# Another layout of the expert lists over the partitions, and another order of POOL's three indirect DMAs

## What is computed

```python
def expert_step(acc, xs):
    wg, wu, wd, g = xs
    h = jax.nn.silu(t @ wg) * (t @ wu)
    return acc + (h @ wd) * g[:, None].astype(t.dtype), None
```

## Time and profile before

| | |
|---|---|
| median of 3 runs | 1410.04 us (1409.48 to 1410.26) |
| the profiled execution | 1410.28 us, its span 1408.4 us |
| PE busy | 1203.7 us, 85% of the span |
| DVE, ACT, POOL busy | 749.5, 529.0, 541.7 us |
| moved by DMA | 329.66 MB, mean 234 GB/s |
| the expert loop (PE's L1870) | about 617 to 1343 us |

### The profile page before, as it was taken

How to read it: one execution, slowest core, us unless ns; L and a number is a source line. 1 busy time by engine, 2 the same in 40 slices (tenths; PEclk the granted TensorE clock), 3 DMA queues, 4 the chain that set the end, 5 groups by cost and what they waited for, 6 DMA issues and landing times. The chain is left out here.

```text
span 1408.4 us, 16199 instructions
## 1 busy us (share of the span) xinstructions
PE 1203.7 (85%) x6611; PEld 950.5 (67%) x6611; DVE 749.5 (53%) x925; ACT 529.0 (38%) x707; POOL 541.7 (38%) x352
## 2 busy tenths in 40 slices
PE   7999788899999999659888988899898888988930
PEld 6999567899998984247666666666666666666620
DVE  3125793532125436337666666666666666666637
ACT  3223672522223120035444444444444444444411
POOL 2001441210010203825555555555555555555413
PEclk9999896899999979979999999999999999999975
DMA  9930601023224075338999999999999998999751
GB/s 276 225 99 29 218 2 68 31 76 104 62 90 178 1 282 208 104 140 329 349 354 347 355 352 348 335 354 356 358 360 359 354 346 344 343 344 350 292 173 69
DMA packets 106017, 329.66 MB, mean 234 GB/s; under 512 B 26866, under 2 KB 59812, under 8 KB 80708
## 3 DMA queue, kind: packets, MB, share of 16 engines
q1 hardware_dynamic: 74848, 265.28, 51.0%
q0 software_dynamic: 30384, 63.02, 13.8%
q10 hardware_dynamic: 708, 0.28, 0.1%
HBM read 324.71 MB, written 49.74 MB: 266 GB/s over the span
## 5 line engine op out<-in xcount | busy, mean ns | idle before, releaser
L838 POOL DMA_INDIRECT yg<-y_rows,idx_all x64 | 258.1, 4033 | 166.4 <-DMA y_rows<-yg,idx_all 160.5
L1510 DVE TENSOR_TENSOR wgu_lo<-wgu,wgu_hi 128x4096 fp32r<-128x4096 f32 x64 | 282.8, 4418 | 0.0
L1125 ACT ACTIVATE wgu_hi<-wgu 128x4096 fp32r<-128x4096 f32 x63 | 227.9, 3617 | 95.4 <-DMA wgu<-in_w_up_e_dram 95.3
L1889 PE MATMUL bank<-wd,hT 128*128 128x512 f32 x512 | 230.1, 592 | 1.3 <-DVE yg L1522 1.3
L1870 PE MATMUL bank<-wgu_hi,xgT 128*128 128x512 f32 x512 | 206.8, 404 | 0.0
L1870 PE MATMUL bank<-wgu_lo,xgT 128*128 128x512 f32 x512 | 201.1, 393 | 0.0
L1870 PE MATMUL bank<-wgu_hi,xgT_lo 128*128 128x512 f32 x512 | 200.3, 391 | 0.0
L1889 PEld LDWEIGHTS bank<-wd,hT 128*128 128x128 f32 x512 | 96.7, 189 | 98.4 <-issue 92.0
L1522 DVE TENSOR_TENSOR yg<-yg,bank 128x512 f32<-128x512 f32 x128 | 82.3, 684 | 149.4 <-PE bank L1889 149.4
L1858 PE MATMUL bank<-ident,xg 128*128 128x128 f32 x512 | 75.1, 291 | 100.0 <-DMA xg<-x_rows,idx_all 97.9
L1502 DVE TENSOR_TENSOR xgT_lo<-bank,xgT 128x512 fp32r<-128x512 f32 x128 | 82.5, 686 | 144.7 <-ACT xgT L1119 144.7
(11 more groups left out here) (274 smaller groups left out, 2263.4 us busy)
## 6 DMA issues: line engine op xcount, KB each, us to landing
wgu<-in_w_gate_e_dram SPq DMA_DIRECT2D x64, 1024.0 KB, 10.2
wgu<-in_w_up_e_dram SPq DMA_DIRECT2D x64, 1024.0 KB, 21.0
wd<-in_w_down_e_dram SPq DMA_DIRECT2D x64, 1024.0 KB, 14.3
raw<-in_w_in_dram SPq DMA_DIRECT2D x16, 1024.0 KB, 5.7
y_rows<-sgln POOLq DMA_DIRECT2D x8, 512.0 KB, 7.1
raw<-in_w_proj_a_dram SPq DMA_DIRECT2D x4, 1024.0 KB, 5.0
raw<-in_w_out_dram SPq DMA_DIRECT2D x4, 1024.0 KB, 4.9
x_lo_kept<-xT_lo SPq DMA_DIRECT2D x1, 2304.0 KB, 10.0
```

Of the source, the lines that this page charges most:

```text
L838: pool.indirect_dma_start(out=yg[i][:], out_offset=None, in_=y_rows[i], in_offset=bass.IndirectOffsetOnAxis(idx, 0), bounds_check=bound, o ...
L1125: act.activation(wgu_hi[u % 2][:], wgu[u % WSLOTS][:], ACT.Copy).then_inc(hi_by_act, 1)
L1510: v.tensor_tensor(wgu_lo[u % WSLOTS][:], w_[:], wgu_hi[u % 2][:].bitcast(F32), ALU.subtract).then_inc(lo_by_dve, 1)
L1889: last = mm(bank[3 + h][:, :], hT[:, u % 2, j, :], wd[slot][:, j, h * 512:(h + 1) * 512], start=j == 0, stop=j == FE // P - 1)
```

## The change

The view `spread` is rearranged: place `s * 64 + q * 16 + c * 2 + h` of a list now goes to partition `h * 64 + s * 32 + c * 4 + q` (`s` and `h` 0 or 1, `q` 0 to 3, `c` 0 to 7). So `idx_all` is loaded in four DMAs of 32 partitions, one for each `h` and `s`, where it was one DMA on POOL (and 16 on SP in the second path). The semaphores' counts follow. On POOL the step's order becomes: gather x of expert `e + 3`, gather y of expert `e`, scatter y of expert `e - 1`, each with the wait that it had.

```diff
-SPREAD = 16
...
-    spread = owner.rearrange("(t b a e) x -> t a b (e x)", t=NT, a=SPREAD, e=E)
+    spread = owner.rearrange("(t s q c h e) x -> t h s c q (e x)", t=NT, s=2, q=4, c=8, h=2)
+    QUARTERS = [(h, s, h * 64 + s * 32) for h in range(2) for s in range(2)]
...
-                    for a in range(SPREAD):
-                        sp.dma_start(idx_all[a * P // SPREAD:(a + 1) * P // SPREAD, :], spread[tile][a]).then_inc(idx_again, 16)
+                    for h, s, p0 in QUARTERS:
+                        sp.dma_start(idx_all[p0:p0 + 32, :], spread[tile][h][s]).then_inc(idx_again, 16)
...
-            pool.dma_start(idx_all[:, :], spread[0]).then_inc(idx_landed, 16)
+            for h, s, p0 in QUARTERS:
+                pool.dma_start(idx_all[p0:p0 + 32, :], spread[0][h][s]).then_inc(idx_landed, 16)
...
-            pool.wait_ge(idx_landed, 16)
+            pool.wait_ge(idx_landed, 64)
...
             for e in range(E):
-                if e >= NACC:
-                    pool.wait_ge(y_put[acc[e]], 16 * (turn[e] - 1))
-                gather_y(acc[e], idx_all[:, e:e + 1])
                 n = e + XGSLOTS - 1
                 if n < E:
                     if e >= 1:
                         pool.wait_ge(h_by_dve, e)
                         pool.wait_ge(ex_xt, e)
                     gather_x(n % XGSLOTS, xg_in[n % XGSLOTS], idx_all[:, n:n + 1])
+                if e >= NACC:
+                    pool.wait_ge(y_put[acc[e]], 16 * (turn[e] - 1))
+                gather_y(acc[e], idx_all[:, e:e + 1])
                 if e >= 1:
                     pool.wait_ge(y_by_dve, 2 * e)
                     scatter_y(acc[e - 1], idx_all[:, e - 1:e])
...
-                    v.wait_ge(idx_again, 16 * SPREAD * tile)
+                    v.wait_ge(idx_again, 64 * tile)
```

## The result

The changed kernel takes 1318.35 us (median of 4 runs, 1317.11 to 1319.55) against 1410.15 us for the kernel before in the same comparison: a ratio of 0.9343, 95% interval 0.9321 to 0.9365. The forecast was 1335 with a range from 1318 to 1372, so the time lies at the very edge of the range (0.9343 of the 1410.28 us from which the forecast starts is 1317.6, just outside it), and the gain of 91.8 us is 16.5 more than the 75.3 forecast. The profiled execution took 1319.55 us, 90.7 less than the one before.

A forecast was written before the change was run, and what follows sets the result against it. The prediction took eight of sixteen DMA engines, each carrying eight rows of each kind, as the bound. From 1410.28 us it took 77.3 for the loop, added 2.0 for the start and 0 for POOL's order: 1335 us, range 1318 to 1372.

The forecast's parts named there:

- the flat rate: Expert loop, from slice 19 on: 329 to 360 GB/s almost without change, read as DMA possibly setting the pace.
- the half-rate stretches: Inside a loop step, 414 GB/s alternates with 221 and 229, read as about half the engines having run dry.
- the sum of 297 KB: Load per step of an engine with eight rows: 196.6 KB weights plus 100.4 KB rows, 11.34 us at 26.2 GB/s.
- the 10.25 us a step: Expert loop with the new layout: 10.1 for DMA plus 0.15 for delays, bounds 10.01 and 10.9; gain 77.3 us.
- The start: Loading the lists ahead of the loop in four issues instead of one: +2.0 us, bounds 0 and +4.
- The POOL order: Gather of x issued 6.7 us sooner in each loop step: cost 0, bounds 0 and 17 us, adding cover.
- The branch that the prediction priced at 17 us: DVE's L1510 stretches x's issue to 4.4 us, so y lands 0.3 us late, 17 us over the loop.
- The landings: Gathers in the loop expected to land 4.6 to 8.4 us after issue with lists spread evenly; then nothing waits.
- Weights late: Rival: gathers take turns with weights on every engine, the loop's step settles at 10.8 us, 1366 us; chance 0.15.
- A rate limit of the memory: Rival: the core is limited to about 360 GB/s, so a loop step takes 11.25 us, 1392 us; chance 0.07.
- The other way round: Rival: an engine owns eight neighbouring partitions, so the new layout is the uneven one, slower at 1526 us; chance 0.04.
- no effect of the layout: Rival: engines not assigned by partition; earlier x gather alone brings 11.34 us a step at best, 1397 us; chance 0.04.

The follow-up runs named there:

- e3: Changed kernel with two of the list's four quarters exchanged, so places 0 to 63 lie on partitions 0 to 63: 1402.02 us, ratio 0.9951 to the kernel before.
- e4: Changed kernel with lists of partitions 4-7 and 32-35 exchanged, meant to give one engine eight of the first 64 places, another none: 1422.12 us.
- e7: Changed kernel with two four-partition groups' lists exchanged, meant to load the neighbour of the otherwise tested engine with eight places: 1424.58 us.
- e6: Kernel before with PE's third gate and up pass (8 of 24 matmuls) left out, all transfers kept: 1391.64 us, ratio 0.988.
- e2: Kernel before with POOL's new order per step (x gather, y gather, scatter), old layout kept: 1400.69 us, ratio 0.9937.
- e5: Changed kernel with PE's third gate and up pass (8 of 24 matmuls) left out, all transfers kept: 1297.42 us, ratio 0.9186 to the kernel before.

## Why the prediction was right and wrong

**What bounds the kernel before: right.** The prediction read eight loaded engines out of the flat rate, the half-rate stretches and the sum of 297 KB. The runs show it: the step follows the busiest engine's rows (e3, e4, e7), not PE's work (e6) and not the order (e2). One slip in it changes no term: the new layout does not put place k on engine k modulo 16. By the rule of the Trainium skill that the prediction cites, place 1 goes to engine 8 and place 2 to engine 1; each engine still gets one of every sixteen places.

**The step that failed: the 10.25 us a step.** It was built as 10.1, because the engines with five rows would need 9.90 at 26.2 GB/s and would reach 98% of that, and 0.15 on top, because a delay would not always be made up with two limits so near each other. Both parts were too much. DMA alone needs 9.81 us a step (e5), which lies between the mean load (9.67) and the busiest engines' (9.90) at 26.2 GB/s: the allowance of 2% isn't there, 259 KB in 9.81 us are 26.4 GB/s. And with 0.2 us between the two limits nothing was lost: every step of the changed kernel takes PE's 10.02 us, 57 of them in 571.4. The 0.23 us too much make 12.9 of the 15.4 us between the forecast and the profiled execution. The prediction had PE's 10.01 as its lower bound, and the value belonged there. That the weights' four slots and gathers issued 16 to 17 us ahead are what makes up a delay is argued; no run has fewer slots.

**The start: mis-sized.** +2.0 was taken, +0.6 measured: three more issues cost 1.7 us and not 2.6, as direct issues follow each other without the 0.30 us of the indirect ones, and the first gather landed 0.9 us sooner, inside the 1.6 allowed for. That is 1.4 us. The remaining 1.1 us are the fifth step, which waits no more (0.6), and the tail (0.5).

**The POOL order: right as a cost of 0, and right that alone it gains next to nothing.** Alone it took 0.6% off, and the wait for x turned into waits for y and weights. The branch that the prediction priced at 17 us, DVE's L1510 catching x's issue and making y late, did come in the run with the order alone, where y was late by 4.3 us a step. In the changed kernel x's issue begins together with that instruction and still takes 1.02 us, and y's is the one stretched, to 4.00. Beside the layout the order is worth nothing that these runs can tell: 1318.98 without it, 1318.35 with it.

**The landings: wrong.** Under 9 us was forecast for the gathers; 11.4 us (x) and 13.4 us (y) were measured. The forecast scaled today's landing by the rows per engine, as if the queue would vanish. It doesn't, because the transfers still need 9.8 of the 10.0 us (e5), and y's 13.4 holds the 4.0 us of its issue. It did no harm, since x and y have 17 and 16 us from issue to need.

**The rivals.** Weights late: ACT waits for none. A rate limit of the memory at 360 GB/s: fell, the core moved 417 GB/s for 490 us. The Trainium skill's sentence that the HBM side binds at about 358 GB/s ("Where 436 GB/s comes from") does not hold for this core running alone; the measurement decides. The other way round, and no effect of the layout: fell with the result and with e3.

## What to carry to other kernels

With gathers and scatters by row, count the bytes of each DMA engine, not of the core: one engine of sixteen with eight rows in place of four or five took back the whole 6.6%. Where everything that comes by DMA is late at once, reordering issues only chooses who waits; look for the engine that is full. And where two limits lie side by side, an allowance for both wants a reason: here, with buffers some steps deep, the time was the larger of the two alone. Cutting the work of the one shows the other.

## What was not expected of the hardware

Sixteen engines level hold 417 GB/s for 490 us, with a fifth of it in rows of 4 KB gathered and scattered. One overloaded engine is slower than eight are, 11.9 against 11.5 to 11.6 us a step at the same load, whichever of two engines it was. In the steps shown, an issue of an indirect DMA on POOL that begins behind the start of DVE's long instruction ends 0.9 us after it: it took 4.40 us in the kernel before, 4.00 in the changed one, 4.87 with the order alone; one that begins together with it takes 1.02. In the run with the old layout and less work on PE, the granted clock over the loop was 0.92, where it was 1.00 with the full work: PE waits there 2.3 us for x in the mean and up to 4.4. One such place (us; PE, PEld, DVE, ACT, POOL busy; clock; DMA share; GB/s):

```profile
1000.00:1002.00 2.00, 0.06 (x1) 0.00 (x0) 1.23 (x2) 2.00 (x1) 1.49 (x2) 1.00 0.83 290
1002.00:1004.00 2.00, 1.06 (x9) 1.07 (x9) 0.00 (x0) 0.29 (x1) 0.51 (x1) 0.94 0.99 406
1004.00:1006.00 2.00, 2.00 (x7) 1.61 (x6) 1.05 (x2) 1.36 (x3) 0.00 (x0) 0.50 1.02 427
```

PE was busy for 0.06 us of the first 2 and for 1.06 of the next, and then the granted clock was 0.50, which is the 1.2 GHz level. The steps of that run are no longer for it (11.42 us against 11.63 in the kernel before).
